# Two on-chip tensors, `u_pad` and `ones`, are declared at another place in the SBUF layout of a two-layer hybrid decoder kernel

## What is computed

```python
for l in range(2):
    h = rmsnorm(x, pre_mix_g[l])
    z = h @ w_in[l]                      # 2560 columns: q, k, v, u, g
    attn = dilated_mixture_attention(rotary(q), rotary(k), v)
    uc = causal_dwconv(u, conv_w[l], conv_b[l])       # 4 taps over time
    rec = gelu(g) * rg_lru(uc, ...)      # gates by 64x64 blocks, then a scan over time
    mixed = concat(rmsnorm(attn), rmsnorm(rec))
    x = x + rmsnorm(mixed @ w_out[l], post_mix_g[l])
    h = rmsnorm(x, pre_ffn_g[l])
    f = swiglu(h, dense...) if l == 0 else moe_ffn(h, router, 8 experts, top 2)
    x = x + rmsnorm(f, post_ffn_g[l])
```

## Time and profile before

| | |
|---|---|
| median of three executions | 1550.37 us |
| the three executions | 1546.11, 1550.42, 1550.37 us |
| the profiled execution: its time | 1546.11 us |
| its span, from the first to the last instruction | 1544.2 us |
| mean granted TensorE clock | 0.971 of full |
| PE busy | 1495.2 us, 97% |
| DVE busy | 1219.2 us, 79% |
| ACT busy | 1019.2 us, 66% |
| share of PE in the chain that ended last | 95% |
| DMA | 437.80 MB, mean 284 GB/s |

### The profile page before, as it was taken

One profiled execution on the slowest core, in us unless ns is written; L12 is line 12 of the kernel. 1 busy time (PEld: TensorE's weight loads), 2 busy tenths in 40 slices (PEclk: granted clock), 3 DMA queues, 4 the chain that ended last, 5 costly groups with the idle time before them and its releaser, 6 DMA issues.

```text
span 1544.2 us, 22425 instructions
## 1 busy us (share of the span) xinstructions
PE 1495.2 (97%) x7892; PEld 1284.0 (83%) x7892; DVE 1219.2 (79%) x1381; ACT 1019.2 (66%) x1209; POOL 21.8 (1%) x45
## 2 busy tenths in 40 slices
PE   7998999998999799999999999999999999999997
PEld 7987999997998688888888888888888888888885
DVE  7765545545676699889899889989888988988997
ACT  6644434444554487777777777778777777777775
POOL 0001000001000100000000000000000000000000
PEclk9969999999997799999999999999999999999998
DMA  9604554554532199989989989989998998998993
GB/s 370 246 13 167 191 191 164 201 187 158 185 137 82 63 355 378 362 327 366 364 319 360 379 317 365 366 334 347 375 360 326 368 364 324 361 378 316 358 379 138
DMA packets 63069, 437.80 MB, mean 284 GB/s; under 512 B 9008, under 2 KB 9136, under 8 KB 10288
## 3 DMA queue, kind: packets, MB, share of 16 engines
q1 hardware_dynamic: 60048, 432.98, 73.7%
q10 hardware_dynamic: 2976, 4.20, 0.8%
HBM read 436.10 MB, written 1.05 MB: 283 GB/s over the span
## 4 chain that ended last, share of the span: by engine, by line
PE 95%; DVE 2%; ACT 1%; issue 0%; DMA 0%; POOL 0%; SPq 0%; DVEq 0%; ACTq 0%
PE psum L414 29%; PE psum L416 29%; PE psum L415 29%; PE psum L664 2%; PE psum L679 2%; PE psum L727 2%; PE psum L548 1%; ACT lru_b L776 0%; PE psum L500 0%; PE psum L559 0%; PE psum L558 0%; DVE xs L1082 0%; DMA con<-consts 0%; DVE hT_lo L991 0%; PE psum L557 0%
## 5 line engine op out<-in xcount | busy, mean ns | idle before, releaser
L980 DVE TENSOR_TENSOR w_lo<-ring,w_hi 128x1024 fp32r<-128x1024 f32 x819 | 956.5, 1221 | 125.9 <-ACT w_hi L763 119.8
L763 ACT ACTIVATE w_hi<-ring 128x1024 fp32r<-128x1024 f32 x819 | 818.0, 1053 | 137.6 <-PE psum L416 134.1
L414 PE MATMUL psum<-w_hi,hT_hi 128*128 128x512 f32 (+1 forms) x1152 | 438.8, 381 | 0.0
L416 PE MATMUL psum<-w_hi,hT_lo 128*128 128x512 f32 (+1 forms) x1152 | 429.6, 373 | 0.0
L415 PE MATMUL psum<-w_lo,hT_hi 128*128 128x512 f32 (+1 forms) x1152 | 428.9, 372 | 0.0
L416 PEld LDWEIGHTS psum<-w_hi,hT_lo 128*128 128x128 f32 x1152 | 217.5, 189 | 38.8
L415 PEld LDWEIGHTS psum<-w_lo,hT_hi 128*128 128x128 f32 x1152 | 217.9, 189 | 37.6 <-issue 1.7
L414 PEld LDWEIGHTS psum<-w_hi,hT_hi 128*128 128x128 f32 x1152 | 217.9, 189 | 37.2 <-DVE w_lo L980 1.7
L414 PE MATMUL psum<-w_hi,act_hi 128*128 128x512 f32 x560 | 218.9, 391 | 0.0
L415 PE MATMUL psum<-w_lo,act_hi 128*128 128x512 f32 x560 | 218.0, 389 | 0.0
L416 PE MATMUL psum<-w_hi,act_lo 128*128 128x512 f32 x560 | 218.0, 389 | 0.0
(11 more groups left out here) (209 smaller groups left out, 857.8 us busy)
## 6 DMA issues: line engine op xcount, KB each, us to landing
ring<-moe_gate SPq DMA_DIRECT2D x114, 1024.0 KB, 6.5
ring<-moe_up SPq DMA_DIRECT2D x114, 1024.0 KB, 6.8
ring<-moe_down SPq DMA_DIRECT2D x112, 1024.0 KB, 6.9
ring<-in_units SPq DMA_DIRECT2D x20, 1024.0 KB, 8.5
ring<-dense_gate SPq DMA_DIRECT2D x14, 1024.0 KB, 4.8
ring<-dense_up SPq DMA_DIRECT2D x14, 1024.0 KB, 4.8
ring<-dense_down SPq DMA_DIRECT2D x14, 1024.0 KB, 4.8
ring<-out_units SPq DMA_DIRECT2D x8, 1024.0 KB, 5.7
```

The costliest lines, as they stand in the source:

```text
L414: pe.matmul(dst, s_hi, m_hi, start=start, stop=False)
L416: return pe.matmul(dst, s_lo, m_hi, start=False, stop=stop)
L763: act.activation(w_hi[:, h % AHEAD, :], ring[:, n % RING, (h % 2) * HCOLS:(h % 2 + 1) * HCOLS], ACT.Copy).then_inc(hi_ready, 1)
L980: dve.tensor_tensor(w_lo[:, h % AHEAD, :], ring[:, (h // 2) % RING, (h % 2) * HCOLS:(h % 2 + 1) * HCOLS], w_hi[:, h % AHEAD, :].bitcast(F3 ...
```

## The change

Two declarations move. `u_pad`, the last tensor of the list, is declared between `qk` and `lru_y`. `ones`, which stood between `blocks` and `con`, is declared behind `rw_lo`. No instruction, no order on any engine, no wait and no DMA is touched.

```diff
@@ -177,6 +177,7 @@
         hT_lo = sb("hT_lo", [P, DK, T], F32R)
         gain = sb("gain", [P, 3, D])
         qk = sb("qk", [P, TT, 2 * AW])
+        u_pad = sb("u_pad", [P, LJ, T + TAPS - 1])
         lru_y = sb("lru_y", [P, LJ, T])
         lru_a = sb("lru_a", [P, LJ, T])
         lru_b = sb("lru_b", [P, LJ, T])
@@ -185,11 +186,11 @@
         act_hi = sb("act_hi", [P, 4, T], F32R)
         act_lo = sb("act_lo", [P, 4, T], F32R)
         blocks = sb("blocks", [P, 2, LJ, P])
-        ones = sb("ones", [P, P])
         con = sb("con", [P, NCON])
         par = sb("par", [P, NPAR])
         rw_hi = sb("rw_hi", [P, DK, EXPERTS], F32R)
         rw_lo = sb("rw_lo", [P, DK, EXPERTS], F32R)
+        ones = sb("ones", [P, P])
         pos_i = sb("pos_i", [P, TT], I32)
         small = sb("small", [P, 4, TT, HALF])
         cs = sb("cs", [P, 2, TT, HALF])
@@ -215,7 +216,6 @@
         item_gate = sb("item_gate", [P, TT, NITEM + 1])
         extra_f = sb("extra_f", [P, 1 + NEXTRA])
         extra_i = sb("extra_i", [P, 1 + NEXTRA], I32)
-        u_pad = sb("u_pad", [P, LJ, T + TAPS - 1])
```

## The result

The changed kernel takes 1558.72 us (median of 6, 1555.27 to 1560.93); the kernel before, timed beside it, 1549.54 us (median of 6, 1546.11 to 1550.71). The ratio is 1.0065, with a 95% interval of 1.0049 to 1.0082: slower by about 10 us. The profiled execution of the changed kernel has a span of 1554.6 us, 10.4 more than the 1544.2 of before.

The account below looks back on a forecast made before the run. PE was taken as the bound, 95% of the chain. All terms were zero, 1546.11 + 0 = 1546.1 us; the spread of executions put the median at 1549.5, likeliest 1545.5 to 1551.5, range 1545 to 1555.5.

Parts of the forecast that it names:

- rival A: Slower: 864 matmuls with moved moving operands begin 7 ns later, 6.0 us, giving 1555.5 us and items of 125.4; chance 0.07.
- part 3: Weight loads of moved tensors, 1680 in the down products: zero, hidden beside the matmul before; 11.8 us if uncovered.
- part 1: Operands far away or in other SBUF regions, price per instruction: zero, as existing DVE, ACT and matmul times hardly vary.
- 819 splits: DVE and ACT splits over slots of `ring`, `w_hi`, `w_lo`, taken as an experiment: address worth at most 12 and 42 ns.
- part 4: Moving operands of moved tensors, 864 matmuls on PE's path: zero, bound 6.0 us at 7 ns each.
- Parts 2, 5 and 6: Operand starts within a row, DVE and ACT operands, DMAs into moved tensors: zero; bounds 7 ns per instruction, 0.7 us, 1.0 us.
- Rival B: Faster: a shift cuts 5 us from each 1.2 GHz stretch in both attention parts, 1544.5 us, 0.32%; chance 0.05.
- the same stretches of low clock: Sign of a right forecast: 1.2 GHz stretches stay; one missing or longer by over 5 us would mean wrong.

Follow-up runs that it names:

- e3: Kernel before with 64 unused bytes ahead of `ring`, so every tensor starts 64 bytes further: ratio 1.0003, items of 124.93 us.
- e2: Kernel before with 64 unused bytes ahead of `act_hi` and 64 behind `act_lo`: ratio 1.007, an item of 126.22 us.
- e4: Kernel before with 384 unused bytes ahead of `ring`, so everything moves together: ratio 1.0000, items of 124.93 us.
- e10: Kernel before with `w_hi`, `w_lo`, `hT` and `act` all 64 bytes further: 1547.30 us in one execution, an item of 124.87 us.
- e8: Changed kernel with 448 unused bytes ahead of `act_hi`: ratio 0.9995, an item of 124.82 us.
- e5: Kernel before with 64 unused bytes ahead of `w_hi` and 448 behind `w_lo`: ratio 0.9985, items of 125.82 us.
- e7: Kernel before with `act_hi` 64, `act_lo` 512 and `hT` 192 bytes further: 1554.42 us in one execution, an item of 126.63 us.
- e12: Kernel before with longer `hT` rooms, used 192 bytes in by all but the experts' tokens, which stay at the start: 1543.88 us, ratio 0.9968.
- e14: Kernel before with longer `hT` rooms, used 64 bytes in by all but the experts' tokens, which stay at the start: 1543.68 us, ratio 0.9961.
- e6: Kernel before with `act_hi` and `act_lo` 256 bytes further, `hT_hi` and `hT_lo` 32 further: 1558.89 us in one execution, an item of 126.83 us.
- e11: Changed kernel with `ones` declared ahead of `con` again: 1557.85 us in one execution, an item of 126.06 us.
- e1: Changed kernel with 64 unused bytes ahead of `act_hi` and 64 behind `act_lo`: ratio 1.0059, an item of 125.85 us.
- e9: Kernel before with 448 unused bytes ahead of `act_hi`: 1548.78 us in one execution, an item of 125.20 us.
- e13: Kernel before with longer `hT` rooms, used 448 bytes in by all but the experts' tokens, which stay at the start: 1544.12 us, ratio 0.9957.

## Why the prediction was wrong

The forecast was no change, 1549.5 us, with a range that reaches at most to rival A's 1555.5; the median is 1558.72.

The step that failed is part 3, weight loads of moved tensors, costed at zero "under the cover" of the matmul before. That a load ends 0.03 us before its matmul begins was read rightly, and the loads did not get longer, 188 ns in both kernels. The error was to take the spare time for proof that nothing about a load can reach the path. What the place of weights and stream to one another costs does not show in the time of the load, but in when the next matmul starts. By the part's own bound, 1680 loads at 7 ns are 11.8 us; 1680 at 6.7 ns are 11.3, and the traces show 9.0 of it in the eight items and 1.7 in the dense part. I had the sum and threw it out, with the reason that it takes over 30 ns per load to get there. It took none. That the 7 ns, taken from DVE's reads of `u_pad`, came so close to PE's 6.7 is luck.

What let it stand was part 1. The 819 splits and the pairs of slots did walk through 112 KB, but in steps of 4096, and `hT_lo` and `act_lo` lie 53,248 = 208 x 256 apart. Every matmul among the rows of the trace before had weights and stream at a distance of 0 modulo 256. It was no experiment on the one quantity that the change moved from 0 to 64; the range should have had both ends of part 3 in it. Of the layout I wrote that all "keep their place in a row of 64 bytes, and lose only their place in one of 128". That is right for each tensor, and e3 shows that no tensor's own place counts. I had not asked for the place of two operands of one instruction to one another.

Rival A had the sign, the place to look (the items) and, by the same luck, the size per matmul (7 ns, measured 6.7), but the wrong operand. The streams that moved, 70 in an item and not 72, stayed at their pace, L679 at 272 ns. The 168 whose weights moved paid. Its 125.4 us per item would have been 126.1 with that count.

L679 speaks only of the stream's own place, not of distances: its weights, `lru_b`, moved by 4160 and its stream, `con`, by 3648, and the difference is 512. The same holds for L727, L500, L548 and L718, whose weights and streams moved by 4160 or by amounts 512 apart. Of the 864 matmuls of part 4 about half changed their distance; in an item these are the 32 of L664 (128 columns, now at 192; the window above counts two at its edge as well), and they start 111.5 ns after one another where it was 111.3. In e2 it is L679 whose distance changed, to 128, and it stays at 108.5 ns (108.4 before). So the 128-column forms don't pay here.

Parts 2, 5 and 6 held. DVE's split is at 1219 ns (1220 before), PE's first wait for `con` is 8.6 us as in the earlier trace rows, and `u_pad`, right beside `lru_y` now, is read as before:

```profile
L1121 DVE SCALAR_TENSOR_TENSOR lru_y<-u_pad,par,lru_y x24: 483/485/486, 29.1 to 408.4; 128x256 f32<-128x256 f32 x24
...
L822 ACT ACTIVATE u_pad<-psum x4: 598/600/602, 23.2 to 404.1; 128x512 f32<-128x512 f32 x4
```

485 ns at a distance of 0 KB and of 39: the 7 ns above L1192 are not the distance. The rule on cachelines of 16 bytes (the Trainium skill, SBUF — State Buffer, Specifications) agrees with that; that it is the cause was not tried.

Rival B, the clock, gave differences of -1.64 and +1.20 us by mixer. The forecast sign "the same stretches of low clock" did not hold: 3.4 us at 1.2 GHz at the second mixer's start where it was 10.2, 27.3 in the first attention part where it was 23.9, and 3.4 more at 15 us. It evens out here, 88 against 90 us in all. What it can do between executions shows in e4, which has the items of before: its profiled execution has 103 us at 1.2 GHz and a span of 1550.9 us, 6.7 more than before, and half of these 13.7 us more at the lower level is 6.8.

For the cause itself the Trainium skill has a statement that the runs do not fit. SBUF — State Buffer, section "Who interferes with whom", gives PE two SBUF read ports, one for the moving operand and one for weight loads, and calls them independent. Here the weight loads stay at 188 ns, but the rate of matmuls depends on how the addresses of the two operands stand to one another: 227 ns at 0 modulo 256, 233 at 64 (e2), and with both moved together no change (e3, e10). The measurement decides; whether it is in the ports that the two meet, no run shows.

Shown: that the place of `act_hi` and `act_lo` against `w_hi` and `w_lo` modulo 256 makes the whole loss (e2 makes it with `u_pad` and `ones` at their old places, e8 takes it away with both at their new ones, e3 and e10 leave only the place of the two to one another). Not shown: what in PE or in SBUF does it.

## What to carry to other kernels

Moving a declaration is a change to every instruction whose operands lie behind it; work out which pairs of operands of one instruction change their place to one another, and not only whether each is aligned. A cover of spare time at an instruction hides its own length and nothing else: when a PE-bound stage has a fixed distance between matmul starts, look at that distance, per form. And before a range in the trace is taken as an experiment ("all slots take the same time"), ask whether the quantity in question varied in it at all.

Where a PE-bound stage has 512-column matmuls of this kind (128x128 weights, both operands in the rounded 32-bit format), try a layout in which weights and stream stand a multiple of 256 bytes apart; it is one line and was worth 9 to 10 us here (e8 against the changed kernel). Other formats and kernels were not tried, and the 256-column form was faster at distances other than 0 (e5 to e7, e12 to e14).

## What the runs showed of the hardware

The mean time between starts of 512-column matmuls at 2.4 GHz, in the three-matmul products of the expert items, worked out from the start times (the few starts that follow a pause left out), with the runs:

| weights minus stream, modulo 256 | ns from start to start | runs, item us |
|---|---|---|
| 0 | 227 | before, e3, e4, e10, e12: 124.87 to 124.93; e8: 124.82 |
| 32 | 233 | e6, weights from `hT`: 126.83 |
| 64 | 233 | after, e2, e11, weights from `act`: 126.05 to 126.22 |
| 128 | 233 | e1, weights from `act`: 125.85 |
| 192 | 229 to 230, uneven by line | e9: 125.20; e5 (all products): 125.82; e7, weights from `hT`: 126.63 with the down products off as well |

The step is 5.5 to 6.7 ns per matmul. Runs of one distance still differ by 0.1 to 0.2 us an item (e8 against before, e2 against the changed kernel), and e5, e7 and e9 show that the split by line does not follow from the distance.

For 256-column matmuls with the stream in `hT` the sign is the other way: 120 ns at a distance of 0 in every trace, and less elsewhere: 116 to 117 at 224 (e6), 117 to 118 at 192 (e14), and at 64 (e5, e7, e12, e13) either 113 to 114 or 117 to 118, by stage.
